# Attention with heads on row halves and rotated parts on row strips, and another order of steps

## The reference, cut to what matters

```python
q_nope, q_rope = q[..., :64], _rope(q[..., 64:], positions)
k_r = jnp.broadcast_to(_rope(k_rope[:, :, None, :], positions), (b, s, 8, 32))
qf = jnp.concatenate([q_nope, q_rope], axis=-1)
kf = jnp.concatenate([k_nope, k_r], axis=-1)
sc = jnp.einsum('bqhd,bkhd->bhqk', qi, k) * scale      # 128 queries at a time
sc = jnp.where(kpos <= qpos, sc, -jnp.inf)
p = jax.nn.softmax(sc, axis=-1)
o = jnp.einsum('bhqk,bkhd->bqhd', p, v)                # 64 channels a head
```

## Time and profile before

| | us |
|---|---|
| median of 3 runs | 3966.22 (3966.11 to 3969.06) |
| profiled execution: span, first to last instruction (its own time is not given beside it) | 3966.9 |
| attention, from the first projection (3142.95) to its end | 607 |
| the last stage, from 3750 | 217 |

### The profile page before, as it was taken

How to read it: one execution, slowest core, us unless ns; L and a number is a source line. 1 busy time by engine, 2 the same in 40 slices (tenths; PEclk the granted TensorE clock), 3 DMA queues, 4 the chain that set the end, 5 groups by cost and what they waited for, 6 DMA issues and landing times. The chain is left out here.

```text
span 3966.9 us, 48763 instructions
## 1 busy us (share of the span) xinstructions
PE 3738.9 (94%) x18907; PEld 1965.7 (50%) x18907; DVE 2256.9 (57%) x3731; ACT 1188.3 (30%) x2336; POOL 791.0 (20%) x714
## 2 busy tenths in 40 slices
PE   6999899999899999999999989899999999999898
PEld 3444454444577774444444434344554365565543
DVE  6688426644466666533227767523555465665578
ACT  3333133455355544511110001111231344444300
POOL 0000000000566655311214332223110000000032
PEclk8999999999999999999999999999999999999999
DMA  5122664476655545411325624321111100000133
GB/s 192 48 48 52 114 132 118 110 132 118 161 183 172 169 138 175 162 34 64 117 85 180 212 101 138 106 85 64 48 38 35 33 1 8 8 1 6 69 117 111
DMA packets 590681, 385.27 MB, mean 97 GB/s; under 512 B 414084, under 2 KB 526824, under 8 KB 587508
## 3 DMA queue, kind: packets, MB, share of 16 engines
q1 hardware_dynamic: 573587, 314.52, 28.8%
q0 software_dynamic: 10336, 42.47, 2.9%
q10 hardware_dynamic: 6528, 25.17, 1.6%
HBM read 251.28 MB, written 130.55 MB: 96 GB/s over the span
## 5 line engine op out<-in xcount | busy, mean ns | idle before, releaser
L667 PE MATMUL bank<-uT,front_W 128*128 128x512 f32 (+1 forms) x1216 | 489.6, 564 | 4.6 <-ACT front_b_ L874 4.6
L599 PE MATMUL bank<-uT,front_W 128*128 128x512 f32 (+1 forms) x896 | 363.6, 564 | 0.0
L667 PEld LDWEIGHTS bank<-uT,front_W 128*128 128x128 f32 x1216 | 232.7, 192 | 253.0 <-issue 246.4
L599 PEld LDWEIGHTS bank<-uT,front_W 128*128 128x128 f32 x896 | 170.0, 191 | 183.2 <-issue 179.9
L3319 PE MATMUL bank<-kT,attn_qT 96*128 96x512 f32 (+3 forms) x640 | 248.4, 540 | 7.4 <-ACT kT L3379 6.8
L1357 POOL TENSOR_TENSOR scan_U<-scan_U,gla_w 128x512 f32<-128x512 f32 x144 | 146.7, 1039 | 168.4 <-DVE scan_U L1545 168.4
L3319 PEld LDWEIGHTS bank<-kT,attn_qT 96*128 96x128 f32 x640 | 114.1, 190 | 130.8 <-issue 74.3
L1768 PE MATMUL bank<-gates_T,gates_S 128*128 128x512 f32 x384 | 172.7, 592 | 0.6 <-POOL uT L1730 0.6
L3439 DVE TENSOR_SCALAR_CACHE_REDUCE attn_sc_big<-bank 128x512 f32<-128x512 f32 (+1 forms) x208 | 125.9, 627 | 73.3 <-PE bank L3319 71.4
L3462 DVE COPY attn_pT<-bank 128x512 f32<-128x512 f32 (+1 forms) x184 | 110.3, 635 | 70.8 <-PE bank L3334 70.8
L1347 POOL TENSOR_TENSOR front_work<-front_work,eGl 128x512 f32<-128x512 f32 x144 | 146.6, 1039 | 10.1 <-DVE front_work L1564 3.6
(11 more groups left out here) (568 smaller groups left out, 7129.1 us busy)
## 6 DMA issues: line engine op xcount, KB each, us to landing
merge_gates<-gates_r ACTq DMA_DIRECT2D x16, 1024.0 KB, 4.1
uT<-merge_gates SPq DMA_DIRECT2D x16, 1024.0 KB, 10.8
gla_asks_keys_values<-front_a SPq DMA_DIRECT2D x14, 1152.0 KB, 10.5
front_W<-in_w_in SPq DMA_DIRECT2D x28, 512.0 KB, 10.6
uT<-in_w_in SPq DMA_DIRECT2D x13, 1024.0 KB, 5.3
scan_dq<-delta_qkv SPq DMA_DIRECT2D x16, 768.0 KB, 5.9
front_work<-gla_asks_keys_values SPq DMA_DIRECT2D x16, 768.0 KB, 7.4
front_work<-delta_qkv SPq DMA_DIRECT2D x16, 768.0 KB, 6.1
```

The source lines that it names most:

```text
L599: m = pe.matmul(bank[:, conv_bank(f, b), 0:n], W[:, f % 2, k, :], uT[:, k, t0:t0 + n], start=(k == 0), stop=(k == KT - 1))
L667: mm = pe.matmul(bank[:, b, 0:n], W[:, s, k, :], uT[:, k, t0:t0 + n], start=(k == 0), stop=(k == KT - 1))
```

## The change

The parts of a head are separated. The plain channels of head `e` lie on partitions `64 e` to `64 e + 63` of one `qT` and one `kT`; the rotated ones have tensors of their own, `kR` with the same key on four strips of 32 partitions and `qR` with tile `(e, r)` on strip `2e + r`. A score tile is now two matmuls into one bank, over 64 rows and over 32 rows. A score step S is 512 keys of all four tiles, each with a bank of its own (four banks, by `2r + e`); the ring for turned exponents has two banks and takes the projections too. Blocks go from 7 down to 0, and the steps of a block's scores are mixed with the groups of the rest of the block before: two chunks turned (T), two of values (V), two and two. Projections are spread over the blocks. VectorE copies odd chunks, and all those of a group that has no score step beside it. The exponents (E) follow the last group that stands beside scores; H are the shares and O the output product.

```diff
-                for e in range(2):
-                    dve.tensor_tensor(kT[R, e, t], kr[R, 0, :], kr[R, 1, :], ALU.add).then_inc(D(f"kr{e}"), 1)
+                for n in range(P // ROPE):
+                    dve.tensor_tensor(kR[n * ROPE:(n + 1) * ROPE, t], kr[R, 0, :], kr[R, 1, :], ALU.add).then_inc(D(f"kr{n}"), 1)
...
-    NS, NTB = 3, 3
+    NTB = 2
     GROUP = 4
-    NPT = 2 * GROUP
-    SC0, TB0, OB0 = 0, 3, 6
+    NPT = 7
+    SC0, TB0, OB0 = 0, 4, 6
...
+        TILES = [(e, r) for r in range(2) for e in range(2)]
+        pieces = lambda p: (p + 2) // 2
+        groups = lambda p: [list(range(2 * p + 2))[c:c + GROUP] for c in range(0, 2 * p + 2, GROUP)]
+        blocks = [(a, p) for a in range(PAIRS) for p in range(TOP, -1, -1)]
+        ahead_of = {(TOP, 0): [("q", 3), ("k", 0)], (TOP, 1): [("k", 1)], (TOP, 2): [("k", 2)], (TOP, 3): [("k", 3)],
+                    (5, 0): [("q", 2)], (3, 0): [("q", 1)], (1, 0): [("q", 0)]}
...
+        def rest_items(b, k, by_vector):
+            a, p = b
+            now, before = groups(p)[k], groups(p)[k - 1] if k else []
+            for h in range(0, max(len(now), len(before)), 2):
+                for c in now[h:h + 2]:
+                    order.append(("T", a, p, c, by_vector or c % 2 == 1))
+                for c in before[h:h + 2]:
+                    order.append(("V", a, p, c))
+        def rest_end(b):
+            order.extend(("V", *b, c) for c in groups(b[1])[-1])
+            order.append(("H", *b))
+        for i, (a, p) in enumerate(blocks):
+            prev = blocks[i - 1] if i else None
+            of_rest = len(groups(prev[1])) if prev else 0
+            for k in range(max(pieces(p), of_rest)):
+                if k < pieces(p):
+                    order += [("P", a, *x) for x in ahead_of.get((p, k), [])]
+                    order.append(("S", a, p, k))
+                if k == 0 and i > 1:
+                    order.append(("O", *blocks[i - 2]))
+                if k < of_rest:
+                    rest_items(prev, k, k >= pieces(p))
+                if k == pieces(p) - 1:
+                    order.append(("E", a, p))
+            if prev:
+                rest_end(prev)
...
         @block.sync
...
                 if a:
-                    sp.wait_ge(TS.sem, TS.at(0, f"k{a - 1}_{NB - 1}"))
+                    sp.wait_ge(TT.sem, TT.at(0, f"q{a - 1}_0"))
...
                 for e in range(2):
-                    sp.dma_start(qT[NOPE:QK, e, :], qr_d[2 * a + e]).then_inc(r_loaded, 16)
+                    for r in range(2):
+                        n = 2 * e + r
+                        sp.dma_start(qR[n * ROPE:(n + 1) * ROPE], qr_d[2 * a + e].rearrange("c (p r t) -> c r p t", r=2, t=P)[:, r]
+                                     ).then_inc(r_loaded, 16)
...
         @block.tensor
...
+            def score(a, p, g):
+                n = score_at[a, p, g]
+                if g == 0:
+                    wait_evicted(pe, f"q{a}_{p // 2}")
+                if p == TOP:
+                    wait_evicted(pe, f"k{a}_{g}")
+                    if g == 0:
+                        pe.wait_ge(r_loaded, 64 * (a + 1))
+                keys = lambda r: slice(g * BANK, min((g + 1) * BANK, length(p, r) * P))
+                spot = lambda e, r: bank[:, SC0 + 2 * r + e, 0:keys(r).stop - keys(r).start]
                 for e, r in TILES:
-                    i = 2 * p + r
-                    for g in range(pieces(p, r)):
...
-                        pe.matmul(bank[:, SC0 + ring[name] % NS, 0:hi - lo], qT[:, e, i * P:(i + 1) * P], kT[0:QK, e, lo:hi],
-                                  start=True, stop=True).then_inc(TS(name), 1)
+                    if n:
+                        b, q, f = scores[n - 1]
+                        pe.wait_ge(DM.sem, DM.at(0, f"s{b}_{q}_{f}_{e}{r}"))
+                    i, rows = 2 * p + r, slice(e * NOPE, (e + 1) * NOPE)
+                    pe.matmul(spot(e, r), qT[rows, i * P:(i + 1) * P], kT[rows, keys(r)], start=True, stop=False)
+                for e, r in TILES:
+                    rows = slice((2 * e + r) * ROPE, (2 * e + r + 1) * ROPE)
+                    pe.matmul(spot(e, r), qR[rows, p, :], kR[rows, keys(r)], start=False, stop=True,
+                              tile_position=((2 * e + r) * ROPE, 0)).then_inc(TS(f"s{a}_{p}_{g}_{e}{r}"), 1)
+            def turned(a, p, c):
+                name = f"t{a}_{p}_{c}"
+                if c == 0:
+                    pe.wait_ge(AE.sem, AE.at(0, f"e{a}_{p}_11"))
+                ring_free(name)
...
         @block.scalar
...
-                        for e in range(2):
-                            m = act.activation(dst[0:NOPE, e, t], bank[e * NOPE:(e + 1) * NOPE, SC0 + ring[name] % NS, :],
-                                               ACT.Copy)
+                act.activation((qT if x == "q" else kT)[:, t], ring_bank(name), ACT.Copy).then_inc(AT(name), 1)
```

More of the change, by code:

```diff
@@ L3197, in phase_attention @@
[L3197 to L3210, removed]
@@ new lines, in phase_attention @@
+        for k in range(len(groups(0))):
+            order.append(("O", *blocks[-2]))
+            rest_items(blocks[-1], k, False)
+        rest_end(blocks[-1])
+        order.append(("O", *blocks[-1]))
+        scores = [it[1:] for it in order if it[0] == "S"]
+        score_names = [f"s{a}_{p}_{g}_{e}{r}" for a, p, g in scores for e, r in TILES]
+        score_at = {x: n for n, x in enumerate(scores)}
+        ring_names = [f"t{it[1]}_{it[2]}_{it[3]}" if it[0] == "T" else f"{it[2]}{it[1]}_{it[3]}" for it in order if it[0] in "TP"]
@@ L3227, in phase_attention @@
[L3227 to L3228 removed]
+        AE = Stages(sem("act_exp"), " ".join(f"e{a}_{p}_{e}{r}" for a, p in blocks for e, r in TILES))
+        AT = Stages(sem("act_turned"), " ".join(n for n in ring_names if n[0] != "t" or not turned_of[n]))
         DT = Stages(sem("dve_turned"), " ".join(n for n in turn_names if turned_of[n]))
@@ new lines, in valued @@
+            def valued(a, p, c):
+                name = f"t{a}_{p}_{c}"
+                wait_evicted(pe, name)
+                if c == 0 and rests.index((a, p)) >= 2:
+                    pe.wait_ge(DO.sem, DO.at(0, "o%d_%d" % rests[rests.index((a, p)) - 2]))
+                r0 = 0 if c < length(p, 0) else P
+                for e in range(2):
+                    h = 2 * a + e
+                    m = pe.matmul(bank[e * DV:(e + 1) * DV, out_bank(a, p), r0:2 * P], vall[:, c, h * DV:(h + 1) * DV],
+                                  pT[:, turn[name] % NPT, e, r0:2 * P], start=(c == 0), stop=(c == 2 * p + 1))
+                m.then_inc(TO(name.replace("t", "o")), 1)
@@ L3404, in rest @@
                     act.wait_ge(DO.sem, DO.at(0, "o%d_%d" % rests[rests.index((a, p)) - 1]))
-                act.activation(spread[:], bank[:, OB0 + rests.index((a, p)) % 2, 2 * P:4 * P], ACT.Copy
-                               ).then_inc(AH_(f"sh{a}_{p}"), 1)
-            scored = None
-            for x, a, p in order:
+                act.activation(spread[:], bank[:, out_bank(a, p), 2 * P:4 * P], ACT.Copy).then_inc(AH_(f"sh{a}_{p}"), 1)
+            for x, *at in order:
                 if x == "P":
-                    project(a)
-                elif x == "S":
-                    if scored:
-                        exponents(*scored, TILES)
-                    scored = (a, p)
-                else:
-                    rest(a, p, scored)
-                    scored = None
+                    project(*at)
+                elif x == "E":
+                    exponents(*at)
+                elif x == "T" and not at[3]:
+                    turned(*at[0:3])
+                elif x == "H":
+                    shares(*at)
         @block.vector
@@ L3421, in _, with score @@
             dve.wait_ge(mask_ready, 2)
-            def scores(a, p):
+            def score(a, p, g):
                 s = slot(p)
-                old = [ap for x, *ap in order[:order.index(("S", a, p))] if x == "R" and slot(ap[1]) == s]
-                if old:
-                    b, q = old[-1]
+                i = blocks.index((a, p))
+                if g == 0 and i >= 2:
+                    b, q = blocks[i - 2]
                     dve.wait_ge(TT.sem, TT.at(0, f"t{b}_{q}_{2 * q + 1}"))
```

246 lines of the change are left out of this document (104 added, 142 removed).

## The result

The median went from 3967.64 us (four runs, 3966.11 to 3970.62) to **4131.02 us** (four runs, 4127.96 to 4133.0), a ratio of 1.0412 with a 95% interval of 1.0397 to 1.0426: slower, as forecast, but by 163 us where the prediction had 103 (4070 against 3966.9), and 11 us beyond the upper end of its range.

What follows compares the result with a forecast made beforehand. TensorE bounds the attention stage, 140.7 of 149.8 us a pair. Streams -13.8, changes of shape +12.0 and waits +28.3 make +26.5 a pair, 106.0 for four, with 0.9 about 107: 4074, said as 4070 us, range 3970 to 4120.

Steps and rivals of the forecast that it cites:

- The streams: Score matmuls on TensorE: halves two at a time, strips four at a time, 44.7 us against 58.5, 13.8 us less a pair.
- the changes of shape: TensorE's array switching between values, halves, strips and transposes: 16.5 us against 4.5, 12.0 us more a pair.
- the cause of the waits: Four score tiles end together and stand ahead of the second chunk's copy in VectorE's queue, so the fourth transpose waits.
- the second and third rivals: Row halves one after another, 4187 us, chance 0.10; strips a third slower, 4.7 us a pair, 4089 us, chance 0.08.
- The waits: TensorE's waits in the attention stage: 42.4 us against 14.1, 28.3 us more a pair, the largest term.
- the sum of units: TensorE's work in one pair before the change, priced by instruction times: 135.7 us, leaving 14.1 us as waits.
- The start of a pair: Block 7's steps wait 0.5 us three times, block 6 waits 1.9 and 3.1 us; projections wait 4.0 us.
- the bound on the waits: Range of the waits term: at least today's 14.1 us a pair; above, no row known for more.
- The first rival: VectorE is in time, waits stay near today's: -1.8 us a pair, 3961 us, not slower; chance 0.17.
- The 3930 at the rival's end: Time the first rival reaches if changes of shape are cheaper; the rival's chance is 0.17.

Runs made afterwards that it cites:

- The filled waits: Against the changed kernel, TensorE makes 5 to 32 unread transposes ahead of a step's fourth chunk, 209 a pair: 4089.77 us, ratio to the kernel before 1.0307.
- early reciprocals: Changed kernel with ScalarE copying odd chunks and projections issued earlier, plus VectorE's reciprocals ahead of the next block's last score step: 3960.36 us, ratio 0.9985.

## Why the prediction was right and wrong

**The streams, the changes of shape and the cause of the waits were right.** Halves run two at a time: the eight instructions from 3572.51 to 3574.43 take 1.92 us, four sets of 0.43 and 0.20 for a change of shape. Strips run four at a time: the eight from 3574.43 to 3575.50 take 1.07 us, two sets and 0.21. The instructions of a set start within 0.02 us. So the second and third rivals fall, and the changes cost about what the sum gave them. By the Trainium skill, "TensorE: Matmul & The Clock Gate", section "Measured speedup vs the span model", each set would have taken about a third longer, 0.14 us, an estimate from its 3.07 times; at 512 columns this trace does not show it. Streams and changes of shape together, -1.8 us a pair in the sum, are -0.9 by the windows, the same as far as two digits of the clock can tell.

**The waits were right in size, 28.3 us more forecast and 27.6 measured, but that they agree so well is luck.** Each wait came out shorter: 0.59 us in a full step (0.8 forecast), 2.43 and 1.21 in last steps (2.85 and 1.6), 1.70 and 0.25 in first ones (2.4). The start of a pair, with the projections 10.6 us by the waits against 10.5, met its size. The level is 36.7 us where 42.4 was forecast, and before it is 9.1 by the windows where 14.1 was counted, so two errors of like size cancel. The 9.1 stood in the earlier trace rows; the other 5.0 are busy time that the sum of units does not cover, though it prices the values 1.3 us too high (0.43 us a chunk, where its row gives 0.41). Of the waits before about 5 us a pair were of transposes for VectorE's copies (20.2 in four pairs), not most of 14.1 as the prediction had it. At the start of a pair the cause was misread: block 7's scores wait 0.75 us each for ScalarE's copy of the keys just projected, not for VectorE's tiles, and before block 6 TensorE waits 3.73 us at the shares, whose reciprocal stands behind block 7's tiles, and not at the transposes.

**The step that failed is the bound on the waits**: "Below, the bound is today's 14.1; above, I know no row for more." The sum priced a wait at its own length and kept every duration beside it at the value of the earlier trace rows, all of the full clock. A wait also made work after it slower: 13.3 us in the third pair, 61 us in the stage (0.11 of 194.0, 0.08 of 191.0, 0.07 of 189.8 and 0.06 of 189.7 us). Some 6 of them were lost before as well, half of the 12 us at 1.2 GHz. The prediction's own sum of 4074 and the other 55 are 4129, against a span of 4126.3. The clock was in view, as a column of the windows in the earlier trace rows. The filled waits show that idle time is the cause: halves, strips and changes of shape are the same there, and the time at 1.2 GHz falls from 123 to 24 us. Where the waits are taken away instead and nothing is added, with early reciprocals, the third pair is at 1.00.

What the lower clock costs can be read without the sum, from lines shown above. From their start to the strips' the halves behind the wait take 3.22 us (3562.99 to 3566.21) and those of the step after 1.92, 1.30 less; the last 2.61 us of the 3.22, from 3563.60 on, lie in the window with the clock at 0.50. The Trainium skill, same page, section "HAM oscillation — how this bites in real kernels", describes this loss, for waits on transfers, and prices it at half of the throttled time. These halves agree: half of 2.61 is 1.30. It was not weighed in the prediction.

**The first rival had its condition right.** It put the time at 3961 if VectorE is in time. With its copies taken away, and with the projections and the reciprocals moved as well, 3960 was measured. That the two meet is in part luck: the rival kept the waits at today's size, and in that kernel's third pair TensorE is idle for 6.3 us and busy for 141.7, against 9.1 and 140.7 before. The 3930 at the rival's end stands without a sum.

## What to carry to other kernels

Price a wait of TensorE twice: its length, and the work behind it at the lower clock if the waits grow long; where they can't go, useful work moved into them, or even useless work, can be cheaper than idling. Taking the waits away was worth more than filling them: 3995 us against 4090. Splitting a matmul over parts of the array makes its results end together, so count what the engine that empties PSUM then has ahead of its other duties. And when a wait is taken away in an in-order queue, look for what stood behind it: five of these experiments moved a wait to the projections or the exponents.

## What was not expected of the hardware

The size of the clock's part, and how little idle time it took. Beside waits of 0.59 us (the steps from 3572.51) the clock stayed full; around waits of 1.7 us and more it fell, though not around each of them, to 1.2 GHz for 123 us of a stage in which TensorE was busy 81% of the time (621.1 of 764.5 us). And 836 transposes that nothing reads shortened the kernel by 41 us.
